# GpSimd in place of VectorE for the low parts of the first mixer's weights

## What is computed

```
def fourier_conv_mixer(h, w_in, conv_w, conv_b, ln_g, ln_b, w_out):
    proj = h @ w_in                                   # 1024 -> 512 u_f, 512 u_v, 512 u_g
    y_f = real(fft2(u_f in 4 groups of 128, over tokens and channels))
    glu = u_v * sigmoid(u_g)
    conv = depthwise convolution of glu, 31 taps, + conv_b
    y_c = silu(layer_norm(conv, ln_g, ln_b))
    return concatenate([y_f, y_c]) @ w_out            # 1024 -> 1024

h = rms_norm(x, mix_norm_g) * (1 + scale) + shift     # shift, scale, gate = cond @ ada_w + ada_b
x = x + gate * fourier_conv_mixer(h, ...)
h = rms_norm(x, ffn_norm_g) * (1 + scale) + shift
x = x + gate * ec_moe(h, ...)                          # 16 experts, 1024 x 1024 gate, up, down
```

## Time and profile before

| what | value |
|---|---|
| median of 3 runs | 3010.8 us (3008.4 to 3011.48) |
| the profiled execution, its own time | 3013.08 us |
| its span, first to last instruction | 3011.8 us |
| TensorE busy | 2464.6 us (82%) |
| VectorE busy | 1116.5 us (37%) |
| ScalarE busy | 801.0 us (27%) |
| GpSimd busy | 3.2 us |
| mean granted TensorE clock | 0.902 |

### The profile page before, as it was taken

The page is one execution under the profiler, slowest core; times in us unless marked ns, Lnnn a source line. Parts: engine busy times, 40 slices in busy tenths (PEclk is TensorE's granted clock), DMA queues, the critical chain, the costliest instruction groups (busy, mean ns, idle before and its releaser), DMA issues.

```text
span 3011.8 us, 31621 instructions
## 1 busy us (share of the span) xinstructions
PE 2464.6 (82%) x13622; PEld 1565.7 (52%) x13622; DVE 1116.5 (37%) x1667; ACT 801.0 (27%) x1140; POOL 3.2 (0%) x7
## 2 busy tenths in 40 slices
PE   7876656767767767667998888889999998887999
PEld 5542111114443111114988454579889774545897
DVE  3740000003551000003544535565455543456554
ACT  3230000002330000003433322544444332324443
POOL 0000000000000000000000000000000000000000
PEclk9988899888878888888999899999999998998999
DMA  8769999997339999999653233356556432424562
GB/s 310 258 232 409 409 409 409 409 409 284 137 132 390 409 409 409 409 409 281 183 185 125 56 94 117 113 139 182 187 159 182 159 112 71 127 84 126 141 182 97
DMA packets 397104, 703.66 MB, mean 234 GB/s; under 512 B 17187, under 2 KB 232483, under 8 KB 396838
## 3 DMA queue, kind: packets, MB, share of 16 engines
q1 hardware_dynamic: 396966, 701.65, 65.5%
HBM read 700.56 MB, written 1.05 MB: 233 GB/s over the span
## 4 chain that ended last, share of the span: by engine, by line
PE 58%; DMA 24%; DVE 7%; SPq 5%; ACT 4%; issue 1%; DVEq 0%; ACTq 0%
PE psum L688 56%; DMA ring<-in_moe_w_down 9%; DMA ring<-in_moe_w_up 7%; DMA ring<-in_moe_w_gate 7%; SPq L558 5%; PE psum L692 2%; DVE arena L1771 2%; ACT ring L1364 1%; DVE lent_r L1771 1%; ACT lent_r L1364 1%; DVE arena L1779 1%; DVE arena L1782 1%; ACT arena L1364 1%; DMA ring<-in_ada_w 0%; DVE arena_r L1771 0%
## 5 line engine op out<-in xcount | busy, mean ns | idle before, releaser
L688 PE MATMUL psum<-ring,arena 128*32 128x512 f32 (+3 forms) x3672 | 686.0, 665 | 288.5 <-DMA ring<-in_moe_w_up 103.3
L688 PE MATMUL psum<-lent_r 128*128 128x256 f32 (+1 forms) x3440 | 641.7, 300 | 23.8 <-DVE lent_r L1771 23.7
L688 PEld LDWEIGHTS psum<-ring,arena 128*32 128x32 f32 (+2 forms) x3672 | 184.4, 130 | 792.6 <-issue 258.2
L688 PEld LDWEIGHTS psum<-lent_r 128*128 128x128 f32 x3440 | 553.8, 196 | 45.2 <-issue 15.6
L688 PE MATMUL psum<-arena_r,lent_r 128*128 128x256 f32 (+1 forms) x1888 | 520.7, 317 | 16.4 <-DVE lent_r L1771 8.5
L1771 DVE TENSOR_TENSOR lent_r<-ring,lent_r 128x2048 fp32r<-128x2048 f32 (+1 forms) x158 | 349.2, 2211 | 285.6 <-ACT lent_r L1364 285.6
L688 PEld LDWEIGHTS psum<-arena_r,lent_r 128*128 128x128 f32 x1888 | 368.5, 196 | 40.1 <-DVE arena_r L1771 9.8
L1364 ACT ACTIVATE lent_r<-ring 128x2048 fp32r<-128x2048 f32 (+1 forms) x158 | 289.7, 1839 | 160.9 <-PE psum L688 160.5
L1364 ACT ACTIVATE arena<-psum 128x512 f32<-128x512 f32 (+3 forms) x118 | 57.8, 501 | 1017.5 <-PE psum L688 955.0
L688 PE MATMUL psum<-ring,hT 128*128 128x512 f32 (+1 forms) x576 | 271.2, 607 | 3.8 <-ACT arena L1364 2.7
L688 PE MATMUL psum<-lent_r,arena_r 128*128 128x512 f32 x1056 | 241.5, 390 | 0.3
(11 more groups left out here) (140 smaller groups left out, 1519.8 us busy)
## 6 DMA issues: line engine op xcount, KB each, us to landing
ring<-in_moe_w_gate SPq DMA_DIRECT2D x128, 1024.0 KB, 18.5
ring<-in_moe_w_up SPq DMA_DIRECT2D x128, 1024.0 KB, 18.6
ring<-in_moe_w_down SPq DMA_DIRECT2D x128, 1024.0 KB, 18.6
ring<-in_ffn_wi SPq DMA_DIRECT2D x176, 512.0 KB, 5.2
ring<-in_ada_w SPq DMA_DIRECT2D x48, 1024.0 KB, 7.5
ring<-in_w_in SPq DMA_DIRECT2D x46, 1024.0 KB, 5.2
ring<-in_ffn_wo SPq DMA_DIRECT2D x44, 1024.0 KB, 4.9
ring<-in_w_out SPq DMA_DIRECT2D x8, 1024.0 KB, 4.9
```

The costliest lines, as they stand in the source:

```text
L688: return T.matmul(out, lhsT, rhs, start=start, stop=stop, **kw)
```

## The change

The eleven subtractions of the first mixer's pieces move from VectorE's list into GpSimd's. They get an event of their own, `fc_low`; TensorE and SyncE wait for it where they waited for `cut_low`. GpSimd does them one after the other behind its first fill, each as soon as ScalarE's `high` is there. All other stages cut as before.

```
-    E.cut_high, E.cut_low = Event(nc, "cut_high", pieces), Event(nc, "cut_low", pieces)
+    E.cut_high, E.cut_low = Event(nc, "cut_high", pieces), Event(nc, "cut_low", [k for k in pieces if k[0] != "fc"])
+    E.fc_low = Event(nc, "fc_cut_low", [k for k in pieces if k[0] == "fc"])
...
+    def low_cut(st, c, p, half):
+        return (E.fc_low if st == "fc" else E.cut_low).at(st, c, p, half)
...
         def piece(st, c, p, *pieces):
-            load((st, c, p), E.cut_low.at(st, c, p, 1), *pieces)
+            load((st, c, p), low_cut(st, c, p, 1), *pieces)
...
                 if n % 2 == 0:
-                    T.wait_ge(*E.cut_low.at("fc", 0, p, 1 if p else 0))
+                    T.wait_ge(*low_cut("fc", 0, p, 1 if p else 0))
...
             gain(0, 0, "mix_norm_g", mods[0], (0, 0))
-            cut("fc", 0, 0, 0)
             shifted_hT(0, mods[0])
-            pieces = cuts("fc", 0, 6)
             taps = itertools.chain(conv(0), conv(1))
             for n, f in enumerate(fc_tiles):
-                if n % 2 == 0:
-                    next(pieces)
...
-            for p in range(6, 8):
-                cut("fc", 0, p)
             for _ in range(CONV_STEPS[1]):
                 next(taps)
...
-            cut("fc", 0, 8)
             V.wait_ge(*E.fc_pe.at(("var", 0)))
...
-                if ch == 1:
-                    cut("fc", 0, 9)
...
     def gpsimd_program():
+        def low(p, half=None):
+            slot = got["fc", 0, p][0]
+            high, out = cut_bufs["fc", 0][p % 2]
+            part = slice(0, SLOT) if half is None else slice(half * SLOT // 2, (half + 1) * SLOT // 2)
+            key = ("fc", 0, p, 1 if half is None else half)
+            G.wait_ge(*E.cut_high.at(*key))
+            G.tensor_tensor(out[:, part], slot[:, part], high[:, part].bitcast(F32), ALU.subtract).then_inc(*E.fc_low.inc(*key))
+
         G.memset(fc.glu, 0.0).then_inc(*E.zeroed.inc("glu"))
+        low(0, 0)
+        low(0, 1)
+        for p in range(1, 10):
+            low(p)
```

More of the change, by code:

```diff
@@ L773, in rows_piece_product @@
             order = [(k, b) for b in range(4) for k in ks] if last else [(k, b) for k in ks for b in range(4)]
[L774 to L777, removed]
+            T.wait_ge(*low_cut(st, c, p, 1 if p else 0))
             for k, b in order:
                 if p == 0 and (k, b) == (1, 0):
-                    T.wait_ge(*E.cut_low.at(st, c, p, 1))
+                    T.wait_ge(*low_cut(st, c, p, 1))
                 tok = slice(b // 2 * P, (b // 2 + 1) * P)
@@ L797, in fourier @@
                 if n % 2 == 0:
-                    T.wait_ge(*E.cut_low.at("fc", 0, p, 1 if p else 0))
+                    T.wait_ge(*low_cut("fc", 0, p, 1 if p else 0))
                 if n == 1:
-                    T.wait_ge(*E.cut_low.at("fc", 0, 0, 1))
+                    T.wait_ge(*low_cut("fc", 0, 0, 1))
                 if n >= 6:
```

## The result

The changed kernel takes 3035.74 us (median of 4 runs, 3033.57 to 3038.09) against 3011.14 us of the kernel before (4 runs): a ratio of 1.0084, with a 95% interval of 1.0066 to 1.0101. The loss of 25 us is five times the +4.5 us of the sum, and lies outside the range. The profiled execution took 3038.09 us, with a span of 3036.8 us; before, the span was 3011.8 us.

The account below looks back on a forecast made before the run. TensorE was taken to set the pace from 48.5 to 118 us, VectorE twice from 116 to 157, then the loads. Shifts carried along the mixer reached +4.5 us at piece 8's product: 3010.8 + 4.5 = 3015.3 us, range 3005 to 3024.

Parts of the forecast that it names:

- the sum: Walk through the first mixer's pieces, adding shifts against the earlier trace: +4.5 us, 3015.3 us as the median.
- step 5: Piece 5: a tap in progress 0.4, GpSimd to 83.0, needed at 81.56 + 1.1; stall 0.4 us, shift +1.5.
- rival (b): VectorE's train of taps doesn't let GpSimd in, holding up pieces 5, 6 and 7: +40 us, 3051; chance 0.10.
- signs of being wrong: Subtraction outside 3.5 to 5.2 us, GpSimd's stretched instead of VectorE's, or experts' first loads not moving with piece 8's product.
- The price of a subtraction: One GpSimd subtraction over 2048 columns, taken as 2.5 passes: 4.4 us, and 2.2 us for a half piece.
- Steps 1 and 2: Opening, piece 0's second half: ready at 48.8, shift +0.3 us; piece 1: GpSimd 48.8 to 53.2, no stall.
- Step 3: Piece 2: GpSimd to 62.0, needed at 61.0 + 0.3; stall 0.8 us, shift +1.1.
- Step 4: Pieces 3 and 4: GpSimd ends at 68.0 and 74.7, needed at 68.8 and 75.7; no stall.
- Blocking in turn: GpSimd and VectorE operations with two SBUF tiles never run together, the later waits for all of the earlier; chance 0.48.
- Step 7: Pieces 6 and 7: output products start at 122.3 instead of 118.46; last tap 138.0 instead of 136.07, shift +2.0.
- step 8: Square root 1.4 us sooner, but normalising products blocked by GpSimd; piece 8's product at 161.35 instead of 156.86, shift +4.5.
- Shifts one to one: A delay of the mixer's end at 156.86 us carries fully through the experts' load stream to the kernel's end.

Follow-up runs that it names:

- e1: Kernel before with only piece 5's subtraction moved to GpSimd, the other ten left on VectorE: 3024.54 us, ratio 1.0051.
- e2: Kernel before with ten subtractions moved to GpSimd, all but piece 5, which stays on VectorE: 3012.05 us, ratio 1.0003.
- e3: Changed kernel with one tiny one-input product in VectorE's list behind the taps of n = 9: 3020.25 us, ratio 1.0031.
- e8: Changed kernel with one tiny one-input product in VectorE's train, eighteen taps after those of n = 9: 3023.84 us (one execution).
- e15: Changed kernel with a tiny one-input product on VectorE behind every convolution step of n = 8 to 11: 3020.17 us, ratio 1.0026.
- e13: Kernel before with only piece 5 on GpSimd, plus a tiny one-input product on VectorE ahead of both steps of n = 8: 3031.72 us.
- e4: Changed kernel with VectorE waiting at n = 10, before its taps, until GpSimd has piece 5: 3018.99 us, ratio 1.002.
- v2: Kernel before with 12 taps moved ahead of the cuts of pieces 6 and 7, and only piece 8 on GpSimd: 3004.23 us, ratio 0.9975.
- e9: Kernel before with only piece 5 on GpSimd, plus a tiny fill on VectorE behind the taps of n = 9: 5232.85 us (one execution).
- e12: Kernel before with only piece 5 on GpSimd, plus a tiny fill on VectorE behind the taps of n = 9, run again: 3011.66 us, ratio 1.0002.

## Why the prediction was wrong

**The failed step is 5**, "a tap in progress 0.4, GpSimd to 83.0", with a stall of 0.4 and a shift of +1.5 in all. It took for granted that whoever comes second waits only for the instruction in progress. That held for VectorE behind GpSimd, and for GpSimd in the first two taps of a run. Piece 5 came in the third, and waited for that and 47 more. Measured: +21.15 us at n = 10 and 1.25 us more through the slower clock. e1 shows that this piece alone loses 12 to 15 us, e2 that the others lose nothing that can be told, e3, e8 and e15 that the wait ends at the first break wherever it is put.

This was rival (b) in mechanism, priced at +40 us with a chance of 0.10. Its own working was wrong twice. The train ended at 98.23 and not at 107, because the second half of the convolution opens with two products with one input: +21 instead of +29. The 46 taps of the earlier trace rows end at 97.68 (79.39 + 18.29) for the same reason; the working counted 76 taps on end. And pieces 6 and 7 weren't locked out a second time: piece 6 came at 138.46, in the last of a run of 12 taps (134.00 to 138.83) behind which VectorE waits for TensorE, and got in there; piece 7 came right behind it, in the first tap of the next run; the two cost 2.5 us, not 10. The rival's argument against itself, that the releases of other engines break the train elsewhere, was right for these two.

The view that should have raised its chance was there: the earlier trace rows shows 46 taps without idle time between them, and step 5's margin was only the 1.1 us that TensorE had in hand. A step that hangs on who gets in, beside a train of 30 us, has a loss of up to 30 us at its end, and 0.10 was too little for it. One of the prediction's own signs of being wrong came true too: here it was GpSimd's record that was stretched, not VectorE's.

**Piece by piece, the rest held.** The price of a subtraction, 4.4 us assumed, was 4.50 to 4.6 us where it got in at once, and 2.35 us for a half (2.2). The Trainium skill's 4497 ns ("GPSIMD Engine Reference", section "Performance versus the Vector engine") agrees with it.

Steps 1 and 2: TensorE started the second half of piece 0 at 50.00 instead of 48.67 us, +1.3 against +0.3 forecast; 0.67 us of that is the trace's own later start. Step 3: a stall of 0.98 us, 0.8 forecast. Step 4: none.

Blocking in turn, the choice in the sum, came out right, though not for the reason given. That VectorE runs near its full rate at 0.40 us for 256 columns misreads the rows: this is 1.6 ns a column, where 2048 columns in 2.29 us are 1.1. What shows the blocking is the traces: a tap beside GpSimd's piece 4 waited for all of it (6.02 us for four), and so did the normalising products beside piece 9 (6.63 us for four, 171.72 on the chain). The Trainium skill ("SBUF — State Buffer", section "Who interferes with whom") says that the second blocks fully, and this part agrees with every trace here. It adds that issue order decides who blocks. Here it does not, from the third tap on: GpSimd was ready at 79.26 us, and the 47 taps that VectorE started after that ran first.

Step 7: the output products +2.5 us of their own against +2.4 worked out (TensorE waits 2.47 us), and step 8: in e2, where piece 5 is out of the way, the product of piece 8 starts 1.5 us late instead of +4.5. The mean's second half was +1.4 there (137.48 against 136.10; +2.0 forecast). The rest is ScalarE's cut 8, which I had let shift by 2.0 with the mean, and which came earlier than before instead: the Sqrt table load behind it is at 147.51 in e2, at 148.16 before, so GpSimd had piece 8 from 147.57 on and not from 150.1. Shifts one to one: in the changed kernel +22.2 at the product of piece 8, +21.8 at the stream, +25.0 at the end. In general this premise did not hold: e1 has +20.0, +16.9 and +11.5 at the same three places, e8 +17.7, +14.6 and +10.7, while e13 has +18.6 at all three. So some 3 us of a shift can be lost before the stream starts, and between the product of piece 8 and the end the traces here differ by -8.5 (e1) to +2.8 us (the changed kernel). These are single traces, and executions of the kernel before alone spread over 16 us, so where that comes from is not settled. Of the 25 us some 3 are of this kind.

**What stays open.** Why the third tap is the limit (number of instructions or time behind the start of the run, the data have 0.65 us on the one side and 0.83 on the other); whether VectorE's being idle ends a lock-out too, as e4 was to show and didn't (piece 6 above got in when its run ended, 2 us ahead of VectorE's next instruction, and so it did in all nine traces that have it on GpSimd, but each time it had come in that run's last tap); what happens to a shift behind the mixer; the last few us of e15.

## What to carry to other kernels

An operation that moves to GpSimd and reads SBUF needs a place on VectorE where it can get in: look not only at the price and the free engine, but at how many VectorE instructions like these taps, with two inputs in SBUF, follow each other without another kind between, because the operation may wait for the whole train, and whoever waits for it waits along. (Only taps of 128 x 256 were tried here.) If such a train can't be avoided, one tiny instruction (0.16 us, or 0.06 for a fill) right behind GpSimd's arrival opens it; better is to move only pieces whose subtraction falls outside any train, as v2 does with piece 8. And a GpSimd record that is five times its siblings is waiting, not working: set it beside VectorE's timeline.

## What the runs showed of the hardware that was not expected

- GpSimd's access to SBUF beside a run of VectorE's two-input taps is won by arrival time: up to 0.65 us behind the run's start it got in within 0.4 us (4.63 to 4.89 us per record against 4.5 undisturbed), from 0.83 us on it waited for the next break, up to 19 us. A one-input copy on GpSimd was kept out too (18.90 us).
- What ended the wait on VectorE's side, each time at once: a one-input product in SBUF of 128 x 256 (held for 4.6 us) or 128 x 2 (4.47), or a fill of 128 x 2, which isn't held itself. A one-input reciprocal from SBUF ran its usual 1.75 us beside GpSimd's piece 8:

```profile
169.93 1.75 DVE L1937 RECIPROCAL arena<-arena 128x256 f32<-128x256 f32 x1 [5.61 <-ACT arena L1367]
```

- The same order of instructions can fall on either side, by 0.2 us. The changed kernel and e4 differ only behind this point, and TensorE's first 84 matmuls took 11.79 us in the one and 10.50 in the other. All four runs of the changed kernel lost about as much (3033.57 to 3038.09), but nothing in its code holds the margin of 0.2 us in place.
- In the one execution of e9, whose kernel is that of e12, the matmuls on the cut buffers took 541 ns on average instead of 301, from end to end, with a recorded granted clock of 1.0; it took 5232.85 us where e12 takes 3011.66. No cause shows in its trace.
